# Second group's u moved and y stored by GpSimd instead of ScalarE, in a streaming encoder layer

## The chip, the cores and the metric

The kernel runs on one core of one Trainium2 chip. Its time is the device time of one execution in microseconds; a smaller number is better. The core has a matrix engine (PE), a vector engine (VectorE, DVE in the rows), a scalar engine (ScalarE, ACT), GpSimd (POOL) and a sync engine (SyncE, SP) that only issues DMAs. DMAs are issued from SP, ACT and POOL queues and carried out by 16 DMA engines that all share.

## The reference

One layer of a hybrid encoder on 512 prompt and 64 sample positions of 2048 features, all in float32:

```
q, k, v, u = split(x @ w_in)
att = rms_norm(band_attention(q, k, v))
ssm = rms_norm(s5(u))        # 64 groups of 16 channels, 64 complex states each; gelu and gate at the end
x1  = layer_norm(alpha * x + concat(att, ssm) @ w_out)
s   = einsum(x1 @ wq, keys)  # 8 heads, 2 halves, 128 keys: top 16 of each, top 16 of their sums
y   = (gelu(x1 . u_tab[idx]) * softmax(top)) @ v_tab[idx]    # 128 experts out of 16384 per position
x2  = layer_norm(alpha * x1 + y)
```

Outputs are x2, the new k and v rows and the last states.

## The kernel before

Positions are dealt into two groups: A with the 64 sample and 128 prompt positions, B with the other 384. Group A runs first, through projections, state space part, attention, w_out, layer norm (tiles 0 and 1) and the expert search. Then B runs the same stages on PE, while VectorE works on the experts of the finished tiles. Every engine has its program written out by hand, in a fixed order, with semaphores between them.

**Slabs.** PE multiplies by 128-column slabs of 1 MB of weights (`slab`, L1556), two buffers, two PSUM banks. SP loads them, in order, among its other loads; a slab waits for its weights and for the copy out of its bank two slabs before (`slab_out`). ScalarE makes these copies (`out_of`, `u_out`). At a width of 384 positions a slab takes about 10.3 us.

**Table rows.** An expert step gathers one row of 2048 float32 from `peer_u` or `peer_v` for each of 128 positions: 1 MB, one indirect DMA on GpSimd (`gather`, L592), one multiply on VectorE (`one_row`, L1360). `ROWS` numbers them 0 to 895. `ring()` gives each row a slot: two slots up to row 15, four from row 16, more later. `gather(i)` waits until the row before in its slot was used, so GpSimd runs two rows ahead of VectorE up to row 15 and four afterwards. VectorE's program has the rows at fixed places: two after each of heads 1 to 7 of tile 0 (`head`, L1265; rows 0 to 13), 28 rows (14 to 41), then one after each of 13 steps of the state scan of B (42 to 54), three ahead of each of the eight heads of tile 1 (55 to 78), 20 rows (79 to 98), and then the first use of y (L1466).

**u of group B.** The eight u slabs of B come as two before the 16 slabs of `N_WA` and six after. The PSUM result of a slab has channels on partitions; the state space matrices want (step, channel) on partitions. So ScalarE stores two slabs at a time to DRAM (`u_store`, L677, four parts) and reads each part back in another layout with eight copies of 48 KB, in runs of 48 numbers, 192 bytes (`u_move`, L682). PE waits for all of them (L1796) before the state products `s_pair`, which are dealt between the matmuls of slabs of v.

**y of group B.** `y_pair` makes y in PSUM between the matmuls of slabs of k and q. After each of four batches of eight pairs ScalarE copies to `U8B` (L931) and issues eight stores of the same shape (L939). SP waits for all 32 (L498) and loads y back as `yB` (L499, 1.5 MB) behind the slab `N_QB + 5`, whose load waits for slab `N_QB + 3`; VectorE waits for it at L1463.

The queue of GpSimd has the row gathers and nothing else in this part of the program.

Of the kernel before, what the change touches and what calls it, by code (L numbers as in the profile page):

```python
# [25 lines left out]
GRP, SG, SN = 64, 16, 64  # L26
SL = 8
# [8 lines left out]
NB = T - NA  # L36
# [32 lines left out]
N_UB = [48, 49, 66, 67, 68, 69, 70, 71]  # L69
N_MA, N_WA = 32, 50  # L70
N_VB, N_KB, N_QB = 72, 80, 88
# [31 lines left out]
def ring():  # L103

    held = [None] * len(SLOT_FROM)
    turns = [0] * len(SLOT_FROM)
    out = []
    for i in range(NR):
        free = [j for j in range(len(SLOT_FROM)) if i >= SLOT_FROM[j]]
        j = min(free, key=lambda j: (-1 if held[j] is None else held[j], j))  # L110
        turns[j] += 1
        out.append((j, turns[j], held[j]))
        held[j] = i
    return out


PLACE = ring()


PARTS = [(0, 0, KK), (1, 0, KK // 2), (2, 0, KK // 2), (2, KK // 2, KK // 2)]  # L120
# [33 lines left out]
def build(nc, a, o):  # L154
    ctx = ExitStack()
    with ctx:
# [405 lines left out]
        @block.gpsimd  # L562
        def _(pool):
            link = Chain(pool, pool_chain)

            pool.wait_ge(ext_done, 1)
            pool.dma_start(escr, ext).then_inc(ext_stored, 16)
            pool.wait_ge(zero_done, 1)
            pool.dma_start(kext.rearrange("(g a) h n -> (a h) g n", a=8)[:, :, 0:7 * SG],
                           zer.rearrange("p (g n) -> p g n", g=8)).then_inc(zeros_stored, 16)  # L570
            pool.wait_ge(ext_stored, 16)
            pool.wait_ge(zeros_stored, 16)
            pool.sem_inc(bias_done, 1)
            pool.wait_ge(tables, 1)
            for g in range(GP):
                wv = lambda t: t[:, :, g, :].unsqueeze(3).to_broadcast([P, 2, NW, SG])
                cvv = lambda t: t[:, g, :].unsqueeze(1).unsqueeze(1).to_broadcast([P, 2, NW, SG])
                if g >= 4:
                    pool.wait_ge(k_done, g - 3)
                    pool.wait_ge(ca_stored[g % 4], 16 * (g // 4))  # L580
                nc.gpsimd.tensor_tensor(tP[0], wv(WrNWi), cvv(Cr), ALU.mult)  # L581
                link(nc.gpsimd.tensor_tensor(tP[1], wv(NWiNWr), cvv(Ci), ALU.mult))
                link(nc.gpsimd.tensor_tensor(CAz[g % 4].rearrange("p r (k h) -> p r k h", k=NW), tP[0], tP[1], ALU.add))
                pool.sem_inc(ca_built, 1)
                link.zero()
            toeplitz(pool, 1)

            pool.wait_ge(y_stored[0], 16 * SL)
            pool.dma_start(yA.rearrange("p (m n) -> p m n", m=8), yscrA.rearrange("(m p) s c -> p m (s c)", p=P)
                           ).then_inc(y_moved[0], 16)  # L590

            def gather(i):  # L592
                kind, t, s = ROWS[i]
                j, turn, before = PLACE[i]
                if i < KK:
                    if s % TOPK == 0:
                        pool.wait_ge(idx_ready, s // TOPK + 1)
                elif s == 0 and kind == "u" or i == R_V3 or i == R_V4:
                    pool.wait_ge(idx_ready, PH + t)
                if before is not None:  # L600
                    pool.wait_ge(used, before + 1)
                elif j < 4:
                    pool.wait_ge(placed, 1)
                    pool.wait_ge(x1_stored, 32)
                    if j >= 2:
                        pool.wait_ge(idx_ready, PH)
                elif j == 4:
                    pool.wait_ge(placed, 2)
                    pool.wait_ge(x1_stored, 32)
                else:  # L610
                    pool.wait_ge(v_stored, 32)
                pool.indirect_dma_start(  # L612
                    out=slot[j], out_offset=None, in_=a["peer_" + kind],
                    in_offset=bass.IndirectOffsetOnAxis(ap=idx[:, t * KK + s:t * KK + s + 1], axis=0)
                    ).then_inc(got[j], 16)

            def e_products(e):
                q = e // EC
                if e % EC == 0 and q >= 4:
                    pool.wait_ge(act_ready, NACT + q - 3)  # L620
                pool.indirect_dma_start(  # L621
                    out=dots[:, 3 * KK + e:3 * KK + e + 1], out_offset=None, in_=ascr,
                    in_offset=bass.IndirectOffsetOnAxis(ap=idxe[:, e:e + 1], axis=0)).then_inc(e_got[q % 4], 16)

            def sum_store(k):
                pool.wait_ge(staged, k + 1)
                pool.dma_start(vscr[k], vstage).then_inc(v_stored, 16)

            for i in range(R_V3 - EAHEAD):
                gather(i)  # L630
                if i == R_V1 + 5:
                    sum_store(0)
                if i == R_U2 + 5:
                    sum_store(1)
            pool.wait_ge(idx_ready, PH + NT - 1)
            for b in range(2):
                pool.wait_ge(a_st[b], 16 * EB // 4)
            for k in range(EAHEAD):
                gather(R_V3 - EAHEAD + k)
                e_products(k)  # L640
            for k in range(NE):
                gather(R_V3 + k)
                if EAHEAD + k < NE:
                    e_products(EAHEAD + k)

        @block.scalar
        def _(act):
# [29 lines left out]
            def u_store(group, uP, uscr, count, lo, hi_, part):  # L677
                act.wait_ge(slab_out, count)
                act.dma_start(uscr.rearrange("(m p) s c -> p m (s c)", p=P)[:, lo:hi_],
                              uP[:, lo:hi_].rearrange("p m s c -> p m (s c)")).then_inc(u_stored[group][part], 16)  # L680
# [151 lines left out]
            def ln1_out(t):  # L832
                t0, n = TILES[t]
                ab, base, banks = (catA, 0, L[2:4]) if t < NGA else (catB, NA, L[0:2])
                for c in range(4):
                    act.wait_ge(x1t_done, 4 * t + c + 1)
                    nc.scalar.copy(half(ab, c)[:, :, t0 - base:t0 - base + n],
                                   banks[c % 2].rearrange("p (q t) -> p q t", q=4)[:, :, 0:n]).then_inc(x1t_out, 1)
                act.dma_start(x1scr[t], x1s[t]).then_inc(x1_stored, 16)
# [41 lines left out]
            def mixed_a(first):  # L881
                for i in range(16):
                    act.wait_ge(slab_done, first + i + 1)
                    src = L[(first + i) % 2]
                    nc.scalar.copy(mixA[:, i, 0:TS], src[:, 0:TS])
                    nc.scalar.copy(mixA[:, i, TS:TS + NA], src[:, 0:NA]).then_inc(slab_out, 1)
# [9 lines left out]
            ln1_stats(1)  # L896
            u_out(N_UB[1], 1, uPB, NB)
            ln1_out(1)
            mixed_a(N_WA)
            scores(0)  # L900
            scores(1)
# [2 lines left out]
            act.wait_ge(x1_ready, 2)  # L904
            for q in range(2, 8):
                u_out(N_UB[q], q, uPB, NB)
                if q == 2:
                    u_store(1, uPB, uscrB, N_UB[1] + 1, 0, 2, 0)
                elif q % 2:
                    u_store(1, uPB, uscrB, N_UB[q] + 1, q - 1, q + 1, q // 2)  # L910
                else:
                    u_move(1, uscrB, U8B, q - 4, q - 2, q // 2 - 2)
            out_of(N_VB, vB[:, 0, :], L[0][:, 0:NB])
            for part in (2, 3):
                u_move(1, uscrB, U8B, 2 * part, 2 * part + 2, part)
            for i in range(1, 4):
                out_of(N_VB + i, vB[:, i, :], L[i % 2][:, 0:NB])
            for b in range(8):
                act.wait_ge(s_done, GP + 4 * b + 4)
# [9 lines left out]
            for b in range(4):  # L929
                act.wait_ge(y_done[1], 8 * b + 8)  # L930
                nc.scalar.copy(U8B[:, 16 * b:16 * b + 16, :].rearrange("p (g a) c -> p a g c", a=2),  # L931
                               low[:, 1024:2048].rearrange("p (a n) -> p a n", a=2)[:, :, 0:8 * CB].rearrange(
                                   "p a (g c) -> p a g c", g=8)
                               ).then_inc(y_out[1], 1)
                if b < 2:
                    out_of(N_KB + 6 + b, kT[:, 6 + b, NA:T], L[b % 2][:, 0:NB])
                act.wait_ge(y_out[1], b + 1)
                for t in range(SL):
                    act.dma_start(yscrB.rearrange("(g h) s c -> s h g c", h=SG)[t][:, 16 * b:16 * b + 16, :],  # L939
                                  U8B[t * SG:(t + 1) * SG, 16 * b:16 * b + 16, :]).then_inc(y_stored[1], 16)  # L940
            for i in range(6):
                out_of(N_QB + i, qB[:, i, :], L[i % 2][:, 0:NB], DH ** -0.5)
            act.wait_ge(yd_ready, 2)
# [1024 lines left out]
```

## Time and profile before

| | |
|---|---|
| median of 3 timed runs | 3700.64 us (3700.53 to 3703.7) |
| the profiled execution, its own time | 3716.53 us |
| its span on the core | 3714.6 us |
| PE, VectorE, ScalarE, GpSimd busy | 66%, 74%, 9%, 33% |
| DMA moved | 1332.41 MB, mean 359 GB/s |
| granted TensorE clock, mean | 0.822 |

The busy share of an engine is an average over stages with different limits, so the stretch between 640 and 1160 us, where u is moved and y stored, is to be read by itself.

### The profile page before, as it was taken

The numbers are of one execution on the slowest core, as the hardware profiler recorded it, in microseconds if no ns is written. First come the engines' busy times: TensorE is split into PE (matmuls) and PEld (weight loads), VectorE is DVE, ScalarE is ACT, GpSimd is POOL, SyncE is SP. The second block draws the span as 40 slices with busy tenths as digits, with TensorE's granted clock in tenths as the row PEclk, the third lists the DMA queues.
The fourth block names the chain that finished last, engine by engine and source line by source line (L and its number), as shares of the span: only waits on it lengthen the run. The fifth ranks groups of instructions, "written<-read, shape, count | busy, mean of one in ns | idle before, by whom it ended". The sixth has DMA issues, their size and how long they took to land.

```text
span 3714.6 us, 30313 instructions
## 1 busy us (share of the span) xinstructions
PE 2464.5 (66%) x11208; PEld 1898.9 (51%) x11208; DVE 2764.5 (74%) x3210; ACT 332.5 (9%) x832; POOL 1237.7 (33%) x1273
## 2 busy tenths in 40 slices
PE   7798799987965776969989999999978000000000
PEld 7687689544733454545577878777767000000000
DVE  5331220979989997787789889985557999999988
ACT  1212211000002221001010000000000000000000
POOL 2420000122123332222222223222222577777772
PEclk9899899998986667989999999999999555555555
DMA  8774355898999999989999999999999999999998
GB/s 248 223 230 124 136 189 187 272 391 331 353 391 344 410 409 383 422 358 397 422 422 423 423 423 423 423 418 423 423 384 410 409 400 408 409 410 383 393 373 350
DMA packets 296882, 1332.41 MB, mean 359 GB/s; under 512 B 69728, under 2 KB 135808, under 8 KB 145312
## 3 DMA queue, kind: packets, MB, share of 16 engines
q0 software_dynamic: 138624, 945.22, 63.1%
q1 hardware_dynamic: 125376, 371.83, 27.1%
q10 hardware_dynamic: 32736, 13.44, 1.4%
q8 instruction: 89, 1.46, 0.2%
q14 instruction: 57, 0.47, 0.0%
HBM read 1282.60 MB, written 57.20 MB: 361 GB/s over the span
## 4 chain that ended last, share of the span: by engine, by line
PE 34%; DMA 25%; DVE 19%; POOL 9%; issue 9%; ACT 1%; SPq 1%; ACTq 1%; DVEq 0%; POOLq 0%
PE low L1561 18%; DMA arena<-in_ut 16%; PE low L1902 10%; DVE arena L1377 6%; POOL arena L612 5%; POOL arena L621 5%; DVE acc L1393 4%; DMA arena<-in_peer_v,arena 3%; DMA arena<-in_w 2%; DMA arena<-in_peer_u,arena 2%; PE low L1635 1%; PE acc L1635 1%; DMA arena<-y_scratch_b 1%; DVE low L1393 1%; DVE arena L1195 1%
## 5 line engine op out<-in xcount | busy, mean ns | idle before, releaser
L1393 DVE SCALAR_TENSOR_TENSOR acc<-arena,acc 128x2048 f32<-128x2048 f32 x443 | 1042.9, 2354 | 266.1 <-DMA arena<-in_peer_v,arena 229.1
L1561 PE MATMUL low<-arena 128*128 128x192 f32 (+1 forms) x4096 | 1063.2, 419 | 102.1 <-DMA arena<-in_w 76.8
L1902 PE MATMUL low<-arena 128*128 128x256 f32 x4096 | 908.8, 383 | 103.3 <-DMA arena<-in_ut 103.2
L1561 PEld LDWEIGHTS low<-arena 128*128 128x128 f32 x4096 | 736.0, 195 | 378.4 <-DMA arena<-in_w 74.4
L1902 PEld LDWEIGHTS low<-arena 128*128 128x128 f32 x4096 | 781.3, 192 | 230.6 <-DMA arena<-in_ut 109.8
L612 POOL DMA_INDIRECT arena<-in_peer_v,arena x576 | 573.4, 995 | 909.2 <-DVE acc L1393 740.9
L1377 DVE SCALAR_TENSOR_TENSOR arena<-arena,acc 128x2048 f32<-128x2048 f32 x320 | 725.0, 2285 | 118.4 <-DMA arena<-in_peer_u,arena 110.9
L612 POOL DMA_INDIRECT arena<-in_peer_u,arena x320 | 320.0, 1000 | 1197.3 <-DVE arena L1377 862.4
L1393 DVE SCALAR_TENSOR_TENSOR low<-arena,low 128x2048 f32<-128x2048 f32 x126 | 296.6, 2354 | 29.6 <-issue 13.6
L621 POOL DMA_INDIRECT arena<-expert_scratch,arena x256 | 260.7, 1018 | 79.2 <-issue 79.2
L873 ACT COPY arena<-low 128x256 f32<-128x256 f32 x128 | 47.6, 372 | 957.5 <-DMA expert_scratch<-arena 635.3
L1687 PE MATMUL low<-arena 128*128 128x128 f32 x320 | 78.9, 403 | 72.3 <-DVE arena L1204 65.2
L1687 PEld LDWEIGHTS low<-arena 128*128 128x128 f32 x320 | 62.8, 283 | 121.1 <-DVE arena L1204 114.0
L1259 DVE MAX8 arena<-arena 128x8 f32<-128x128 f32 (+1 forms) x120 | 40.5, 338 | 97.8 <-ACT arena L847 94.8
L1195 DVE CUSTOM_DVE_ANT_0 arena<-acc,arena 128x128 f32<-128x128 f32 (+1 forms) x24 | 10.6, 447 | 114.4 <-PE acc L1665 78.5
L670 ACT COPY arena<-low 128x384 f32<-128x384 f32 (+1 forms) x80 | 34.3, 430 | 620.4 <-PE low L1561 598.5
L1109 DVE TENSOR_TENSOR arena<-arena 128x256 f32<-128x256 f32 x32 | 15.5, 484 | 99.1 <-PE acc L1608 98.6
L1240 DVE SCALAR_TENSOR_TENSOR arena<-arena,acc 128x2048 f32<-128x2048 f32 x2 | 4.6, 2289 | 98.3 <-PE acc L1748 98.3
L1671 PE MATMUL low<-arena 64*128 64x256 f32 (+2 forms) x96 | 66.8, 797 | 13.6 <-DVE arena L1195 9.6
L1713 PE MATMUL low<-arena 128*64 128x128 f32 x320 | 73.3, 388 | 0.0
L865 ACT ACTIVATE arena<-arena 128x16 f32<-128x16 f32 x16 | 3.5, 216 | 682.2 <-DMA arena<-expert_scratch,arena 391.6
L581 POOL TENSOR_TENSOR arena<-arena 128x288 f32<-128x288 f32 x32 | 22.6, 705 | 112.2 <-DMA c_scratch<-arena 83.1
(274 smaller groups left out, 1688.0 us busy)
## 6 DMA issues: line engine op xcount, KB each, us to landing
arena<-in_w SPq DMA_DIRECT2D x128, 1024.0 KB
arena<-in_ut SPq DMA_DIRECT2D x128, 1024.0 KB
expert_scratch<-arena SPq DMA_DIRECT2D x64, 256.0 KB
arena<-in_peer_v,arena POOLq DMA_INDIRECT x576
arena<-toeplitz_scratch SPq DMA_DIRECT2D x64, 128.0 KB, 4.1
arena<-c_scratch SPq DMA_DIRECT2D x64, 128.0 KB, 4.7
bias_scratch<-distance_scratch SPq DMA_DIRECT2D x1, 5120.0 KB, 23.2
x_scratch<-arena ACTq DMA_DIRECT2D x5, 1024.0 KB
```

What stands on the lines that cost most here:

```text
L612: pool.indirect_dma_start(out=slot[j], out_offset=None, in_=a["peer_" + kind], in_offset=bass.IndirectOffsetOnAxis(ap=idx[:, t * KK + s:t ...
L621: pool.indirect_dma_start(out=dots[:, 3 * KK + e:3 * KK + e + 1], out_offset=None, in_=ascr, in_offset=bass.IndirectOffsetOnAxis(ap=idxe[: ...
L873: nc.scalar.copy(astg[j // 2 % 2].rearrange("p u (i t) -> p i u t", i=2)[:, j % 2], L[j % 4][:, 0:NSD].rearrange("p (u t) -> p u t", u=2)) ...
L1195: nc.vector.tensor_tensor_reduce(S[0:rows, 0:keys], src, bias, -1.0, HIGHEST, ALU.add, ALU.min, accum_out=stat[0:rows, 0:1]).then_inc(mn_r ...
L1377: stt(slot[j], slot[j], 1.0, acc[:, :], ALU.mult, ALU.mult, accum_out=dots[:, t * KK + s:t * KK + s + 1]).then_inc(used, 1)
L1393: stt(held, slot[j], wv_, held, ALU.mult, ALU.add).then_inc(used, 1)
L1561: ins = mm(L[n % 2][:, 0:width], wring[n % 2][:, k, :], rhs(k), start=k == 0, stop=k == KT - 1)
L1635: ins = mm(d, CAy[g % 8][hf(g2), r, :], Hs[hf(g2), r, g, 0:width], start=False, stop=r == 1)
L1671: ins = mm(L[u % 2][:, 0:n], qB[hf(hh), m, P * (j - 1):P * j], kT[hf(hh), m, TS:TS + n], start=True, stop=True)
L1687: ins = mm(L[2][:, P * k:P * k + P], S[:, P * k:P * k + P], dg, start=True, stop=True)
L1713: ins = mm(d, vs, PT[:, P * k:P * k + P], start=k == 0, stop=k == j)
L1902: ins = mm(L[j % 4][:, 0:NSD], ud[j % 4][:, k, :], lane(catB, k)[:, P:NB], start=k == 0, stop=k == KT - 1)
```

## The change

GpSimd gets two functions, `u_move(part)` and `y_store(b)`, and calls them at set places of its loop over rows: part 0 of u ahead of row 0, parts 1, 2 and 3 ahead of rows 2, 4 and 8, and the four batches of y ahead of rows 70, 77, 84 and 91. ScalarE no longer issues these 64 copies. Its store of part 0 of u moves up, behind the second layer norm; the stores of parts 1 to 3 stay behind the copies of slabs 3, 5 and 7 of u.

```diff
--- before.py
+++ after.py
@@ -115,6 +115,10 @@
 
 
 PLACE = ring()
+
+
+U_ROWS = [2, 4, 8]
+Y_ROWS = [70, 77, 84, 91]
 
 
 PARTS = [(0, 0, KK), (1, 0, KK // 2), (2, 0, KK // 2), (2, KK // 2, KK // 2)]
@@ -589,6 +593,20 @@
             pool.dma_start(yA.rearrange("p (m n) -> p m n", m=8), yscrA.rearrange("(m p) s c -> p m (s c)", p=P)
                            ).then_inc(y_moved[0], 16)
 
+            def u_move(part):
+                pool.wait_ge(u_stored[1][part], 16)
+                pool.wait_ge(x1_ready, 2)
+                for k in range(SL):
+                    pool.dma_start(U8B[k * SG:(k + 1) * SG, 16 * part:16 * part + 16],
+                                   uscrB.rearrange("(g h) s c -> s h g c", h=SG)[SL - 1 - k][:, 16 * part:16 * part + 16]
+                                   ).then_inc(u_moved[1], 16)
+
+            def y_store(b):
+                pool.wait_ge(y_out[1], b + 1)
+                for t in range(SL):
+                    pool.dma_start(yscrB.rearrange("(g h) s c -> s h g c", h=SG)[t][:, 16 * b:16 * b + 16, :],
+                                   U8B[t * SG:(t + 1) * SG, 16 * b:16 * b + 16, :]).then_inc(y_stored[1], 16)
+
             def gather(i):
                 kind, t, s = ROWS[i]
                 j, turn, before = PLACE[i]
@@ -626,7 +644,12 @@
                 pool.wait_ge(staged, k + 1)
                 pool.dma_start(vscr[k], vstage).then_inc(v_stored, 16)
 
+            u_move(0)
             for i in range(R_V3 - EAHEAD):
+                if i in U_ROWS:
+                    u_move(U_ROWS.index(i) + 1)
+                if i in Y_ROWS:
+                    y_store(Y_ROWS.index(i))
                 gather(i)
                 if i == R_V1 + 5:
                     sum_store(0)
@@ -896,6 +919,7 @@
             ln1_stats(1)
             u_out(N_UB[1], 1, uPB, NB)
             ln1_out(1)
+            u_store(1, uPB, uscrB, N_UB[1] + 1, 0, 2, 0)
             mixed_a(N_WA)
             scores(0)
             scores(1)
@@ -904,16 +928,9 @@
             act.wait_ge(x1_ready, 2)
             for q in range(2, 8):
                 u_out(N_UB[q], q, uPB, NB)
-                if q == 2:
-                    u_store(1, uPB, uscrB, N_UB[1] + 1, 0, 2, 0)
-                elif q % 2:
+                if q % 2:
                     u_store(1, uPB, uscrB, N_UB[q] + 1, q - 1, q + 1, q // 2)
-                else:
-                    u_move(1, uscrB, U8B, q - 4, q - 2, q // 2 - 2)
-            out_of(N_VB, vB[:, 0, :], L[0][:, 0:NB])
-            for part in (2, 3):
-                u_move(1, uscrB, U8B, 2 * part, 2 * part + 2, part)
-            for i in range(1, 4):
+            for i in range(4):
                 out_of(N_VB + i, vB[:, i, :], L[i % 2][:, 0:NB])
             for b in range(8):
                 act.wait_ge(s_done, GP + 4 * b + 4)
@@ -934,10 +951,6 @@
                                ).then_inc(y_out[1], 1)
                 if b < 2:
                     out_of(N_KB + 6 + b, kT[:, 6 + b, NA:T], L[b % 2][:, 0:NB])
-                act.wait_ge(y_out[1], b + 1)
-                for t in range(SL):
-                    act.dma_start(yscrB.rearrange("(g h) s c -> s h g c", h=SG)[t][:, 16 * b:16 * b + 16, :],
-                                  U8B[t * SG:(t + 1) * SG, 16 * b:16 * b + 16, :]).then_inc(y_stored[1], 16)
             for i in range(6):
                 out_of(N_QB + i, qB[:, i, :], L[i % 2][:, 0:NB], DH ** -0.5)
             act.wait_ge(yd_ready, 2)
```

GpSimd's order where row gathers begin (`in_peer_u` gathers, the first two being rows 0 and 1; `u_scratch_b` copies are the moves of u; in brackets the semaphores waited for), before:

```order
L589 DMA arena<-y_scratch_a 128x8x192 [waits y_stored_a]
L612 DMA arena<-in_peer_u,arena 128x2048 [waits x1_stored,x1_placed,idx_ready]
L612 DMA arena<-in_peer_u,arena 128x2048 [waits x1_stored,x1_placed]
L612 DMA arena<-in_peer_u,arena 128x2048 [waits row_used] x14
L612 DMA arena<-in_peer_u,arena 128x2048 [waits x1_stored,idx_ready,x1_placed]
L612 DMA arena<-in_peer_u,arena 128x2048 [waits idx_ready,x1_stored,x1_placed]
```

and in the changed kernel:

```order
L593 DMA arena<-y_scratch_a 128x8x192 [waits y_stored_a]
L600 DMA arena<-u_scratch_b 16x16x48 [waits x1_ready,u_stored_b0]
L600 DMA arena<-u_scratch_b 16x16x48 x7
L630 DMA arena<-in_peer_u,arena 128x2048 [waits x1_stored,x1_placed,idx_ready]
L630 DMA arena<-in_peer_u,arena 128x2048 [waits x1_stored,x1_placed]
L600 DMA arena<-u_scratch_b 16x16x48 [waits x1_ready,u_stored_b1]
L600 DMA arena<-u_scratch_b 16x16x48 x7
L630 DMA arena<-in_peer_u,arena 128x2048 [waits row_used] x2
L600 DMA arena<-u_scratch_b 16x16x48 [waits x1_ready,u_stored_b2]
L600 DMA arena<-u_scratch_b 16x16x48 x7
L630 DMA arena<-in_peer_u,arena 128x2048 [waits row_used] x4
L600 DMA arena<-u_scratch_b 16x16x48 [waits x1_ready,u_stored_b3]
```

The sixteen rows stood in one run; now moves stand ahead of rows 0, 2, 4 and 8, and each part first waits for its store, `u_stored_b`.

GpSimd's order further on, from row 64 (the single gathers with `idx_ready` are rows 64, 80 and 96, the first of a head's sixteen), before:

```order
L612 DMA arena<-in_peer_u,arena 128x2048 [waits row_used,idx_ready]
L612 DMA arena<-in_peer_u,arena 128x2048 [waits row_used] x15
L612 DMA arena<-in_peer_u,arena 128x2048 [waits row_used,idx_ready]
L612 DMA arena<-in_peer_u,arena 128x2048 [waits row_used] x15
L612 DMA arena<-in_peer_u,arena 128x2048 [waits row_used,idx_ready]
```

and in the changed kernel (`y_scratch_b` copies are the stores of y):

```order
L630 DMA arena<-in_peer_u,arena 128x2048 [waits row_used,idx_ready]
L630 DMA arena<-in_peer_u,arena 128x2048 [waits row_used] x5
L607 DMA y_scratch_b<-arena 16x16x48 [waits y_out_b]
L607 DMA y_scratch_b<-arena 16x16x48 x7
L630 DMA arena<-in_peer_u,arena 128x2048 [waits row_used] x7
L607 DMA y_scratch_b<-arena 16x16x48 [waits y_out_b]
L607 DMA y_scratch_b<-arena 16x16x48 x7
L630 DMA arena<-in_peer_u,arena 128x2048 [waits row_used] x3
L630 DMA arena<-in_peer_u,arena 128x2048 [waits row_used,idx_ready]
L630 DMA arena<-in_peer_u,arena 128x2048 [waits row_used] x3
L607 DMA y_scratch_b<-arena 16x16x48 [waits y_out_b]
L607 DMA y_scratch_b<-arena 16x16x48 x7
```

Before there were only gathers here; now a group of eight stores stands ahead of rows 70, 77 and 84 (and another, not shown, ahead of row 91), each behind a wait for ScalarE's copy of y.

ScalarE's order from the copy of slab 5 of u, before (`arena<-low` are its copies out of PSUM):

```order
L670 COPY arena<-low 128x384 [waits slab_done]
L679 DMA u_scratch_b<-arena 128x2x384 [waits slab_out]
L670 COPY arena<-low 128x384 [waits slab_done]
L685 DMA arena<-u_scratch_b 16x16x48 [waits u_stored_b1]
L685 DMA arena<-u_scratch_b 16x16x48 x7
L670 COPY arena<-low 128x384 [waits slab_done]
L679 DMA u_scratch_b<-arena 128x2x384 [waits slab_out]
L670 COPY arena<-low 128x384 [waits slab_done]
L685 DMA arena<-u_scratch_b 16x16x48 [waits u_stored_b2]
L685 DMA arena<-u_scratch_b 16x16x48 x7
L685 DMA arena<-u_scratch_b 16x16x48 [waits u_stored_b3]
L685 DMA arena<-u_scratch_b 16x16x48 x7
```

and now:

```order
L693 COPY arena<-low 128x384 [waits slab_done] x2
L702 DMA u_scratch_b<-arena 128x2x384 [waits slab_out]
L693 COPY arena<-low 128x384 [waits slab_done] x2
L702 DMA u_scratch_b<-arena 128x2x384 [waits slab_out]
L693 COPY arena<-low 128x384 [waits slab_done] x4
L937 COPY arena<-low 128x4x2x48 [waits s_done] x2
L693 COPY arena<-low 128x384 [waits slab_done]
L937 COPY arena<-low 128x4x2x48 [waits s_done] x2
```

The moves and their waits are gone, and the copies and stores follow each other.

## Rows read from the trace of the kernel before

**Rows 1.** DMA view: busy share in 40 slices; issues, KB each, us to landing.

```profile
DMA  8774355898999999989999999999999999999998
...
arena<-in_ln_g SPq DMA_DIRECT2D x3, 1024.0 KB, 4.7
```

**Rows 2.** Busy time by stretch; columns as in the header line.

```profile
core 0: us, PE busy (x) PEld busy (x) DVE busy (x) ACT busy (x) POOL busy (x), PEclk, DMA share, GB/s
...
680.00:720.00 40.00, 40.00 (x125) 23.56 (x124) 37.04 (x102) 1.92 (x4) 5.62 (x6) 1.00 0.85 273
760.00:800.00 40.00, 35.19 (x213) 18.55 (x214) 27.58 (x25) 3.38 (x7) 12.39 (x14) 0.91 1.02 413
...
1200.00:1300.00 100.00, 74.54 (x256) 48.54 (x256) 98.50 (x155) 22.81 (x57) 34.67 (x37) 0.62 0.99 402
1500.00:1600.00 100.00, 100.00 (x312) 58.92 (x311) 71.82 (x31) 6.32 (x12) 28.27 (x31) 1.00 1.01 422
```

**Rows 3.** Chain of work, pieces in order of time, 600 to 1160 us.

```profile
753.89 2.31 DVE arena L1377 x2
...
849.66 0.86 DVE arena L1134
...
923.39 0.91 PE low L1561 x2
...
1059.16 34.31 DMA arena<-y_scratch_b
```

**Rows 4.** Timeline of VectorE: rows 84, 98, and the first use of y.

```profile
1045.18 2.29 DVE L1377 SCALAR_TENSOR_TENSOR arena<-arena,acc 128x2048 f32<-128x2048 f32 x1 [1.47 <-DMA arena<-in_peer_u,arena]
...
1088.54 2.29 DVE L1377 SCALAR_TENSOR_TENSOR arena<-arena,acc 128x2048 f32<-128x2048 f32 x1 [0.79 <-DMA arena<-in_peer_u,arena]
...
1093.49 2.21 DVE L1466 SCALAR_TENSOR_TENSOR arena<-arena 128x384 f32<-128x384 f32 x4 [2.65 <-DMA arena<-y_scratch_b]
```

**Rows 5.** Timeline of ScalarE with its DMA issues (ACTq), 660 to 745 us.

```profile
671.75 0.38 ACTq L679 DMA_DIRECT2D u_scratch_b<-arena  x1
...
692.39 0.38 ACTq L679 DMA_DIRECT2D u_scratch_b<-arena  x1
...
713.03 0.42 ACTq L679 DMA_DIRECT2D u_scratch_b<-arena  x1
...
722.85 15.81 ACTq L685 DMA_DIRECT2D arena<-u_scratch_b  x16
```

**Rows 6.** Timeline of ScalarE: last y copy, its DMA issues, next copy.

```profile
1024.06 10.45 ACTq L939 DMA_DIRECT2D y_scratch_b<-arena  x8
1034.55 0.87 ACT L672 ACTIVATE arena<-low 128x384 f32<-128x384 f32 x2 [10.52 <-issue]
```

**Rows 7.** Tensor u_scratch_b: issue to landing of its stores, min/median/max.

```profile
DMA to landing us min/median/max: 8.2/9.3/11.0
```

**Rows 8.** Timeline of GpSimd: issues of small copies and row gathers.

```profile
211.86 8.95 POOL L367 DMA_DIRECT2D toeplitz_scratch<-kernel_scratch  x16 [6.74 <-DMA kernel_scratch<-arena]
...
656.94 1.03 POOL L612 DMA_INDIRECT arena<-in_peer_u,arena  x1 [311.81 <-DVEq L1327]
...
669.56 0.94 POOL L612 DMA_INDIRECT arena<-in_peer_u,arena  x1 [10.31 <-DVE arena L1377]
```

**Rows 9.** Timeline of GpSimd: row gathers 83, 84 and 91.

```profile
1034.88 0.94 POOL L612 DMA_INDIRECT arena<-in_peer_u,arena  x1 [8.25 <-DVE arena L1377]
1037.09 0.94 POOL L612 DMA_INDIRECT arena<-in_peer_u,arena  x1 [1.27 <-DVE arena L1377]
...
1056.11 0.94 POOL L612 DMA_INDIRECT arena<-in_peer_u,arena  x1 [2.47 <-DVE arena L1377]
```

**Rows 10.** Timeline of VectorE: rows 2 and 4 of the first head stage.

```profile
681.48 2.29 DVE L1377 SCALAR_TENSOR_TENSOR arena<-arena,acc 128x2048 f32<-128x2048 f32 x1 [0.24 <-DVE arena L1325]
...
695.96 2.29 DVE L1377 SCALAR_TENSOR_TENSOR arena<-arena,acc 128x2048 f32<-128x2048 f32 x1 [0.24 <-DVE arena L1325]
```

**Rows 11.** Timeline of PE: the first state product.

```profile
754.34 0.44 PE L1806 MATMUL low<-arena 128*64 128x48 f32 x8
```

## Prediction

> **What bounds the kernel now.** I read the DMA view first. The busy share of the DMA engines is at 9 in nearly every slice after the first two fifths [rows 1]. The windows then say what kind of stretch each one is [rows 2]. From 680 to 720 us VectorE is busy 37.0 of 40 us and DMA 0.85: the first head stage (top-16 search, decode, and two table rows after each of heads 1 to 7) is VectorE's. From 760 to 800 DMA is at 1.02 and VectorE at 27.6 of 40: gathers and weights share the bandwidth. From 1200 to 1300 VectorE is busy 98.5 of 100 with DMA at 0.99, and from 1500 to 1600 DMA is at 1.01: the later stages have no slack on one of the two. All that follows the first group is one long VectorE program with the table rows dealt into it in fixed places, so a microsecond that VectorE loses before 1160 us comes back only where gathers are the limit and somebody else gave them bandwidth.
>
> The chain of work between 750 and 1160 us has four parts [rows 3]: VectorE ends rows 12 and 13 at 756.2, then takes rows 14 to 41 as they land, until 849.66 (93.5 us for 28 rows, 3.3 us each, where one multiply takes 2.3); VectorE's scan steps run from 849.66 until the state is ready, when PE starts the y pairs at 923.39; last stands the load of y, 34.31 us from 1059.16. VectorE waited for that load only 2.65 us [rows 4].
>
> The copies that the change moves cost nobody else much today. ScalarE issues the moves of u between its copies; the longest piece is sixteen issues, 15.81 us from 722.85 [rows 5], while PE has two banks ahead. Only the last eight stores of y hurt: their issue holds ScalarE from 1024.06 for 10.45 us, and the copy that frees PE's bank starts at 1034.55 after 10.52 us of idleness by issue [rows 6].
>
> **The change part by part.** Removed from ScalarE: 32 moves and 32 stores. Added to GpSimd, in order, among the row gathers: eight moves ahead of row 0, then ahead of rows 2, 4 and 8, and eight stores ahead of rows 70, 77, 84 and 91. GpSimd works in order, so a gather behind a move also waits for what the move waits for.
>
> Part 0 of u is stored ahead of the sixteen slabs that come before the first head stage, and row 0 is gathered only at 656.94 [rows 8]: nothing lost. Part 1 is not stored until ScalarE has copied slab 3: the store is issued at 671.75 [rows 5] and lands 9.3 us later, the median of four (8.2 to 11.0) [rows 7], at 681.1. Only then can GpSimd issue the eight moves. A plain copy of 256 short pieces on GpSimd shows as 8.95 us for sixteen, 0.56 each [rows 8]: 4.5 us, until 685.6. Gather 2, which before was issued at 669.56 [rows 8], starts then. From issue to the multiply that needs it I take 8.1 us, from gather 84 (issued at 1037.09 [rows 9], multiply at 1045.18 after a wait for it [rows 4]). Row 2 starts at 693.7 instead of 681.48 [rows 10]: 12.2 us late.
>
> Part 2 does not depend on that delay, since PE and ScalarE run on: store issued at 692.39, landed at 701.7, moves issued by 706.2, gather 4 landed at 714.3. Row 4 started at 695.96 before [rows 10]: **18.3 us late**, and this contains the 12.2. In this stage only two slots take rows, so nothing is fetched ahead and VectorE stands. Bounds of this term: lowest 692.39 + 8.2 + 4.5 + 4.7 (a load of 1 MB into SBUF, alone in its queue [rows 1]) = 709.8, 13.8 us late; highest 692.39 + 11.0 + 7.5 (eight at a gather's 0.94) + 10.1 (gather 0, issued at 656.94 [rows 8], was there for its row at 667.0, 14.48 before row 2) = 721.0, 25.0 us late.
> Part 3: store at 713.03, landed 722.3, moves issued by 726.8. Gather 8 has to wait for row 6 anyway, which starts one step (695.96 - 681.48 = 14.5 us) after row 4, at 728.8. It costs nothing; without that cover it would be up to 4.5.
>
> A rule to weigh here: the row says that a gather of 1 MB takes 8.1 us to its use, beside other traffic [rows 4, 9]. The Trainium skill, page "DMA: Bandwidth & Descriptors", section "Anatomy of one DMA — SWDGE (gpsimd) path", gives a fixed 2.0 us plus the bytes at 436 GB/s, an estimate of 4.4 us for this gather. With it row 4 would be 14.6 us late instead of 18.3. The row was taken in a saturated stretch and this stage has 0.85, so the truth may lie between; the sum keeps the row.
>
> Is it taken back? PE has its moved u in time (part 3 is issued by 726.8, and the first state product ran at 754.34 [rows 11]), so PE starts the state products on time and draws its slabs and tables 18 us ahead of VectorE. In the stretch of 28 rows the demand beside the gathers is then a little higher: PE could have up to 3 MB more done by row 41, and 3 MB at the stretch's 413 GB/s [rows 2] are 7 us. Lower bound 0, if the queues share as before and 3.3 us per row stays. I take **+2 us** (nearer to 0, since PE waits for weights there too). VectorE then reaches the scan about 20 us late, the state is ready about 20 us late, and PE's y pairs start late by the same.
>
> The stores of y, in times that leave out this shift. GpSimd idles 8.25 us between triples of gathers in the second head stage [rows 9], which hides the 4.5 us of the first two groups of stores (rows 70, 77); uncovered they would cost 4.5 each. The third group is issued behind gather 83, from 1035.8 to 1040.3, so gather 84 goes 3.2 us later than at 1037.09 [rows 9], and its row has waited for it before [rows 4]: about 3 us. The fourth stands ahead of gather 91. GpSimd idled 2.47 us before that one at 1056.11 [rows 9], so it is issued from 1053.6 + 3 to 1061, and lands behind the gathers in front of it, 8.1 us on, near 1069.5. The y load can start then, 10 us later than its 1059.16. On the other side ScalarE is free at 1024.06, PE runs its next slabs 10.5 us earlier, and the 1 MB slab issued just before the y load is out of its queue. If the 34.31 us were for 1 + 1.5 MB, the 1.5 MB alone take 20.6: y lands between 1090 and 1104, middle 1097. Row 98 ended near 1090.8 [rows 4], now near 1094. VectorE starts on y at 1097 instead of 1093.49: **+3 us** (from -3, the old wait gone, to +11).
>
> Sum: 18.3 + 2 + 3 = 23 us. Behind it VectorE and PE are both late at the same point of the program and nothing in the later stages is idle enough to absorb it. The profiled execution took 3716.5 us and its span 3714.6; it is 15.9 us above the median of 3700.64 of the timed runs. So 3739.5 in a profiled run, and 3700.6 + 23 = **3723 us** in timed ones.
>
> **Rivals.**
> 1. *Likeliest: the late gathers 2 and 4.* Bounds 13.8 + 0 - 3 = +11 to 25 + 7 + 11 = +43; with the terms not all at one end, +12 to +33, so 3713 to 3734. Chance 0.63.
> 2. *The stall is taken back in rows 14 to 41, and PE's 10.5 us are a gain.* One mechanism: while VectorE stands, PE's side gets its tables and slabs, and the gathers then find the bandwidth free. It decides from where 28 rows take 93.5 - 18.3 = 75 us or less, 2.7 us each; the floor is 2.3, so it is possible. Then VectorE is on time, the y wait of 2.65 us goes, and part of PE's 10.5 us fills DMA time: 0 to -7 us, 3694 to 3700. Against it: DMA is at 1.02 there, the amount to be moved is the same, and from 754 to 773 the engines would be partly idle, which nothing refunds. Faster than by 0.2%: 0.08. Taken back in part, so that it ends within 7.4 us: 0.11.
> 3. *y comes later still:* the last stores queue behind four gathers, land near 1080, and the y load again takes 34 us, to 1114. VectorE has only two rows to do meanwhile. 18 + 2 + 20 = +40, 3735 to 3745. For it: the y load was slow beside gathers [rows 3]. Against it: GpSimd stops gathering when VectorE stands, which frees the bandwidth. Chance 0.12.
> 4. *Short landings:* the moves and gathers in the half-empty stage take 5 us rather than 8, and the y part costs nothing: +8 to +12, 3709 to 3713. Chance 0.06.
>
> **How the numbers follow.** Slower by over 0.2% (7.4 us, about what a measurement of this kernel can tell): 0.63 + 0.12 + 0.06 = 0.81; within it 0.11; faster 0.08. The range goes from 3704, which takes in half of the partly absorbed cases, to 3740, which takes in half of rival 3; some 0.12 is left out by the chances of the cases, and the rest of the two tenths stands for unknown costs inside them.
>
> **What would show it.** GpSimd: a wait of about 22 us ahead of the moves before gather 2, ended by the store of u, and gather 2 near 686, gather 4 near 706. VectorE: idle before rows 2 and 4, together 18 us (14 to 25), none before rows 6 and 8; scan near 870 instead of 849.66; PE's first y pair near 943. ScalarE: no idleness by issue at 1034. The y load issued about 30 us after its old time, shorter than 34 us, and VectorE's wait for it 3 to 10 us. The forecast is wrong if gather 2 is not held by the store, if rows 14 to 41 take under 80 us, or if the lateness at 1160 is not found at the end.

## The result, and the profile after

The changed kernel takes 3719.75 us (median of 6 runs, 3714.09 to 3725.89) against 3702.26 us (6 runs, 3700.53 to 3707.18): ratio 1.0045 (95% interval 1.0032 to 1.0058), so 16.7 us slower (12 to 21). Its profiled execution took 3725.89 us, span 3723.9.

Timeline of GpSimd in the changed kernel, first head stage (start and length in us; in brackets the idle time before and what ended it). L600 are moves of u, L630 row gathers. It is to be read against [rows 8]; this execution runs 1.5 us later than that of before from the start of the stage (first search of head 0 at 648.31 instead of 646.77).

```profile
679.65 4.56 POOL L600 DMA_DIRECT2D arena<-u_scratch_b  x8 [18.87 <-DMA u_scratch_b<-arena]
684.51 1.01 POOL L630 DMA_INDIRECT arena<-in_peer_u,arena  x1 [0.30 <-issue]
...
703.09 4.57 POOL L600 DMA_DIRECT2D arena<-u_scratch_b  x8 [16.28 <-DMA u_scratch_b<-arena]
707.96 1.01 POOL L630 DMA_INDIRECT arena<-in_peer_u,arena  x1 [0.30 <-issue]
...
726.82 4.56 POOL L600 DMA_DIRECT2D arena<-u_scratch_b  x8 [6.26 <-DMA u_scratch_b<-arena]
732.17 1.02 POOL L630 DMA_INDIRECT arena<-in_peer_u,arena  x1 [0.80 <-DVE arena L1390]
```

The stores it waits for land after 6.1, 8.9 and 12.0 us, against 8.2 to 11.0 in [rows 7] (DMA view of three short windows, KB each, us to landing):

```profile
u_scratch_b<-arena ACTq DMA_DIRECT2D x1, 384.0 KB, 6.1
```

```profile
u_scratch_b<-arena ACTq DMA_DIRECT2D x1, 384.0 KB, 8.9
```

```profile
u_scratch_b<-arena ACTq DMA_DIRECT2D x1, 384.0 KB, 12.0
```

GpSimd waits 18.87 us for the store of part 1 and 16.28 us for that of part 2, with gathers 2 and 4 queued behind. It had idled there before too (10.31 us before gather 2 [rows 8]), so the loss is less than the wait: gather 2 goes 13.4 us late (684.51 against 669.56, less the 1.5). VectorE in the same stage, rows 2, 4 and 6, against [rows 10]:

```profile
691.50 2.29 DVE L1390 SCALAR_TENSOR_TENSOR arena<-arena,acc 128x2048 f32<-128x2048 f32 x1 [8.65 <-DMA arena<-in_peer_u,arena]
...
714.17 2.29 DVE L1390 SCALAR_TENSOR_TENSOR arena<-arena,acc 128x2048 f32<-128x2048 f32 x1 [8.08 <-DMA arena<-in_peer_u,arena]
...
729.33 2.29 DVE L1390 SCALAR_TENSOR_TENSOR arena<-arena,acc 128x2048 f32<-128x2048 f32 x1 [0.24 <-DVE arena L1338]
```

It stands 8.65 us before row 2 and 8.08 us before row 4, where it had 0.24 before, and does not stand before row 6. In the windows the stretch that had VectorE at 37.0 of 40 us [rows 2] now has 21.4, and DMA 0.75 instead of 0.85:

```profile
680.00:720.00 40.00, 40.00 (x126) 23.57 (x125) 21.40 (x52) 1.92 (x4) 14.06 (x22) 1.00 0.75 243
760.00:800.00 40.00, 40.00 (x263) 21.24 (x262) 30.15 (x54) 3.37 (x7) 10.41 (x12) 1.00 0.92 351
```

In this trace nothing of it comes back in rows 14 to 41: the first scan step (in [rows 3] at 849.66) is at 868.64, so 17.4 us later beside the 1.5. The third and fourth group of stores of y (L607) and the gathers behind them, against [rows 9]:

```profile
1053.80 0.94 POOL L630 DMA_INDIRECT arena<-in_peer_u,arena  x1 [8.24 <-DVE arena L1390]
1054.74 1.80 POOL L607 DMA_DIRECT2D y_scratch_b<-arena  x3
1057.38 2.78 POOL L607 DMA_DIRECT2D y_scratch_b<-arena  x5 [0.83 <-issue]
1060.46 1.00 POOL L630 DMA_INDIRECT arena<-in_peer_u,arena  x1 [0.30 <-DVE arena L1390]
...
1076.11 0.94 POOL L630 DMA_INDIRECT arena<-in_peer_u,arena  x1 [2.47 <-DVE arena L1390]
1077.05 4.56 POOL L607 DMA_DIRECT2D y_scratch_b<-arena  x8
1081.91 1.01 POOL L630 DMA_INDIRECT arena<-in_peer_u,arena  x1 [0.30 <-issue]
```

Gather 84 is issued at 1060.46, and VectorE waits 5.28 us for it where it waited 1.47 [rows 4]. Below are row 84, row 98 and the first use of y (1114.11, L1479). It has no bracket: VectorE does not wait for y any more, and row 98 before it is the one that comes late.

```profile
1067.64 2.29 DVE L1390 SCALAR_TENSOR_TENSOR arena<-arena,acc 128x2048 f32<-128x2048 f32 x1 [5.28 <-DMA arena<-in_peer_u,arena]
...
1111.90 2.29 DVE L1390 SCALAR_TENSOR_TENSOR arena<-arena,acc 128x2048 f32<-128x2048 f32 x1 [1.29 <-DMA arena<-in_peer_u,arena]
1114.11 2.20 DVE L1479 SCALAR_TENSOR_TENSOR arena<-arena 128x384 f32<-128x384 f32 x4
```

The y load goes at 1087.55, 28.4 us after its old time [rows 3]; SP has been waiting since 1068.7 for the stores. It lands 26.1 us after its issue (34.3 before), near 1113.7, only 0.5 us ahead of its use. ScalarE's 10.52 us of idleness by issue [rows 6] are gone.

```profile
1068.30 0.43 SPq L501 DMA_DIRECT2D out_h<-arena  x1
1087.55 0.38 SPq L503 DMA_DIRECT2D arena<-y_scratch_b  x1
```

To follow a lateness through the program I take the start of one gather in each profile, less the start of the first search of head 0 (646.77 before, 648.31 here), and subtract the same of before. Gather 756 is issued at 3311.8 before and 3335.2 here: 2686.9 - 2665.0 = 21.9 us late. It had been 21.1 at gather 224 (1463.8 and 1486.4): what is late there is still late almost 2000 us further on. The profiled executions end only 9.4 us apart because that of before lost 14 us behind gather 756 (373.5 us to the last gather, 359.4 in the changed kernel) in code that is the same; its 3716.53 us lie above all other timed runs of before (3707.18 at most).

### The profile page after: what moved, and what is told of

Its sections match the earlier page's. It is cut to its first block, busy times and chain, and to the rows that moved or that the text cites. A ratio compares the mean times of both kernels' runs of the same rounds, so it can differ in the third digit from the quotient of the medians.

```text
span 3723.9 us, 30317 instructions
## 1 busy us (share of the span) xinstructions
PE 2473.7 (66%) x11208; PEld 1905.9 (51%) x11208; DVE 2764.5 (74%) x3210; ACT 333.1 (9%) x832; POOL 1247.5 (33%) x1337
## 4 chain that ended last, share of the span: by engine, by line
PE 33%; DMA 32%; DVE 22%; POOL 6%; issue 5%; ACT 1%; ACTq 0%; SPq 0%; DVEq 0%; POOLq 0%
PE low L1574 18%; DMA arena<-in_ut 17%; PE low L1915 10%; DMA arena<-in_peer_v,arena 9%; DVE arena L1390 8%; DMA arena<-in_peer_u,arena 3%; DVE acc L1406 3%; POOL arena L630 3%; POOL arena L639 3%; DMA arena<-in_w 2%; DVE low L1406 1%; PE acc L1648 1%; DVE arena L1208 1%; DMA arena<-bias_scratch 1%; PE acc L1621 1%
## 5 line engine op out<-in xcount | busy, mean ns | idle before, releaser
L630 POOL DMA_INDIRECT arena<-in_peer_v,arena x576 | 561.4, 975 | 926.0 <-DVE acc L1406 788.2
L630 POOL DMA_INDIRECT arena<-in_peer_u,arena x320 | 320.9, 1003 | 921.1 <-DVE arena L1390 806.1
L639 POOL DMA_INDIRECT arena<-expert_scratch,arena x256 | 245.2, 958 | 78.3 <-issue 78.3
L600 POOL DMA_DIRECT2D arena<-u_scratch_b x32 | 18.1, 592 | 258.1 <-DMA u_scratch_b<-arena 258.1
L1684 PE MATMUL low<-arena 64*128 64x256 f32 (+2 forms) x96 | 69.7, 829 | 12.4 <-DVE arena L1208 8.4
## 6 DMA issues: line engine op xcount, KB each, us to landing
expert_scratch<-arena SPq DMA_DIRECT2D x64, 256.0 KB, 26.1
```

Of the source, the lines that this page charges most:

```text
L630: pool.indirect_dma_start(out=slot[j], out_offset=None, in_=a["peer_" + kind], in_offset=bass.IndirectOffsetOnAxis(ap=idx[:, t * KK + s:t ...
L639: pool.indirect_dma_start(out=dots[:, 3 * KK + e:3 * KK + e + 1], out_offset=None, in_=ascr, in_offset=bass.IndirectOffsetOnAxis(ap=idxe[: ...
L1684: ins = mm(L[u % 2][:, 0:n], qB[hf(hh), m, P * (j - 1):P * j], kT[hf(hh), m, TS:TS + n], start=True, stop=True)
```

## The experiments

Each was compared with the kernel before on the same chip, 6 to 12 runs against 27 to 29. The table gives the lateness in us against the profile of before, worked out as above, at the issue of four gathers, at the first scan step, at the issue of the y load, and at "y use", VectorE's first instruction on y. Each column but the last comes from one profiled execution:

| run | gather 16 | first scan step | gather 84 | gather 91 | y load | y use | gather 756 | timed ratio (95%) |
|---|---|---|---|---|---|---|---|---|
| changed kernel | 17.8 | 17.4 | 21.8 | 24.3 | 26.8 | 19.1 | 21.9 | 1.0045 (1.0032 to 1.0058) |
| e1, u only | 15.7 | 13.9 | 13.9 | 12.2 | 14.1 | 14.2 | 14.9 | 1.0043 (1.0028 to 1.0059) |
| e6, u part 1 only | 9.6 | 9.5 | 9.4 | 7.8 | 9.8 | 9.9 | 13.9 | 1.0030 (1.0018 to 1.0042) |
| e2, y only | 0.0 | 0.1 | 5.0 | 9.4 | 11.7 | 3.7 | 7.4 | 1.0012 (1.0001 to 1.0023) |
| e8, y, third group at 80 | -0.1 | 0.1 | 0.0 | 4.0 | 7.4 | -0.8 | 0.8 | 0.9998 (0.9984 to 1.0013) |
| e3, u at 4, 8, 10 | 0.4 | 0.7 | 4.8 | 8.2 | 10.0 | 1.9 | 2.9 | 1.0006 (0.9995 to 1.0016) |
| e7, copies first | -0.1 | 0.1 | 0.0 | 2.9 | -12.8 | 2.9 | 2.2 | 0.9999 (0.9989 to 1.0009) |

**e1_u_only.** The changed kernel with the stores of y given back to ScalarE:

```diff
             for i in range(R_V3 - EAHEAD):
...
-                if i in Y_ROWS:
-                    y_store(Y_ROWS.index(i))
...
+                act.wait_ge(y_out[1], b + 1)
+                for t in range(SL):
+                    act.dma_start(yscrB.rearrange("(g h) s c -> s h g c", h=SG)[t][:, 16 * b:16 * b + 16, :],
+                                  U8B[t * SG:(t + 1) * SG, 16 * b:16 * b + 16, :]).then_inc(y_stored[1], 16)
```

> The changed kernel with the stores of y back on ScalarE; only the moves of u are on GpSimd, ahead of rows 0, 2, 4 and 8. Theory (VectorE stands before rows 2 and 4 because the moves wait for u's stores): the whole stall of the changed kernel is here, 8 to 9 us before row 2 and about 8 before row 4, gather 84 late by 17 to 18 us; ScalarE's 10.5 us of idleness by issue is back. Time 17 us (12 to 21) above the kernel before, ratio 1.0046. Rival (the loss of the changed kernel is made mostly by the stores of y on GpSimd): under 7 us above.

Measured 3719.69 against 3706.59 us, ratio 1.0043 (1.0028 to 1.0059): 16 us by the ratio. VectorE stands 9.09 us before row 2 and 6.12 before row 4:

```profile
688.28 2.29 DVE L1392 SCALAR_TENSOR_TENSOR arena<-arena,acc 128x2048 f32<-128x2048 f32 x1 [9.09 <-DMA arena<-in_peer_u,arena]
...
708.90 2.29 DVE L1392 SCALAR_TENSOR_TENSOR arena<-arena,acc 128x2048 f32<-128x2048 f32 x1 [6.12 <-DMA arena<-in_peer_u,arena]
```

The moves of u make most of the loss; the rival with under 7 us falls. The times can't tell this run from the changed kernel (1.0043 and 1.0045). Of the 15.7 us at gather 16 it has 13.9 left at the first scan step, so here rows 14 to 41 gave 1.8 us back.

**e6_part1_only.** As e1, with parts 2 and 3 where their stores have landed:

```diff
-U_ROWS = [2, 4, 8]
+U_ROWS = [2, 8, 10]
```

> The moves of u on GpSimd ahead of rows 0, 2, 8 and 10, the stores of y on ScalarE: of the two stalls only the one of part 1 is left. Theory: VectorE waits 8 to 9 us before row 2 and not before row 4, and the lateness of 8 to 9 us stays to the end: ratio 1.0023 (1.0012 to 1.0035). Rival (a lateness of this size in the head stage is taken back while rows 14 to 41 wait for DMA): under 3 us.

Measured 3715.86 against 3704.4 us, ratio 1.0030 (1.0018 to 1.0042), 11 us. VectorE's rows 2 and 4:

```profile
691.66 2.29 DVE L1392 SCALAR_TENSOR_TENSOR arena<-arena,acc 128x2048 f32<-128x2048 f32 x1 [9.25 <-DMA arena<-in_peer_u,arena]
...
706.39 2.29 DVE L1392 SCALAR_TENSOR_TENSOR arena<-arena,acc 128x2048 f32<-128x2048 f32 x1 [0.24 <-DVE arena L1340]
```

One stall of 9.25 us before row 2, and 0.24 before row 4. Gather 16 is 9.6 us late and the first scan step 9.5, so rows 14 to 41 give nothing back here though they wait for DMA. Gather 756 is 13.9 us late, not 9.9 as the use of y. Of these 4 us, 2.6 come between gathers 200 and 224 (10.2 and 12.8 late), and so do 1.6 in the changed kernel, 3.3 in e2 and 2.3 in e10, while e1, e3 and e4 lose nothing there. Why is not settled, so lateness behind gather 200 is good to some 3 us only.

**e3_u_late.** The changed kernel with one list of numbers changed:

```diff
-U_ROWS = [2, 4, 8]
+U_ROWS = [4, 8, 10]
```

> The changed kernel with the moves of parts 1, 2 and 3 ahead of rows 4, 8 and 10 in place of 2, 4 and 8, where the store has landed before GpSimd comes there (or nearly: part 3's store lands near 724, gather 10 goes at 727.5). Theory: no wait of VectorE before rows 2 to 13 beyond 1 us, so only the cost of y stays: +2 to +6 us, as the run with y only. Rival (it is the eight issues and the packets on the gathers' queue that cost, not the wait for the store): each moved group still costs 4 to 5 us, +12 to +18 us.

Measured 3706.89 against 3706.59 us, ratio 1.0006 (0.9995 to 1.0016), which is 2 us (-2 to +6). The moves of part 1 still wait for the store, but with gathers 2 and 3 ahead of them:

```profile
682.19 4.55 POOL L600 DMA_DIRECT2D arena<-u_scratch_b  x8 [8.68 <-DMA u_scratch_b<-arena]
687.05 1.01 POOL L630 DMA_INDIRECT arena<-in_peer_u,arena  x1 [0.30 <-DVE arena L1390]
```

Gather 4 goes 2.2 us later than before and VectorE does not stand before any of the rows 2 to 13. The same 24 issues are on the same queue, so the issues and their packets cost nothing that these runs can resolve: the wait for the store did. The rival with 4 to 5 us a group falls.

**e2_y_only.** The kernel before with `y_store` and its call as in the changed kernel, and ScalarE's stores taken out:

```diff
+Y_ROWS = [70, 77, 84, 91]
...
             for i in range(R_V3 - EAHEAD):
+                if i in Y_ROWS:
+                    y_store(Y_ROWS.index(i))
                 gather(i)
```

> The kernel before with only the stores of y on GpSimd, ahead of rows 70, 77, 84 and 91. Theory: gather 84 late by about 4 us, the y load issued some 5 to 10 us later than at 1059, VectorE late by 2 to 5 us at 1160; time +2 to +6 us, ratio 1.0005 to 1.0016. Rival (ScalarE's freed 10.5 us are a gain for PE that reaches the end): -3 to -7 us.

Measured 3710.38 against 3706.59 us, ratio 1.0012 (1.0001 to 1.0023), 4.4 us. Below are gather 83, the third group and gather 84 on GpSimd, then rows 83 and 84 (L1384) and the first use of y (L1473) on VectorE:

```profile
1040.13 0.94 POOL L621 DMA_INDIRECT arena<-in_peer_u,arena  x1 [9.57 <-issue]
1041.07 4.56 POOL L598 DMA_DIRECT2D y_scratch_b<-arena  x8
1045.93 1.01 POOL L621 DMA_INDIRECT arena<-in_peer_u,arena  x1 [0.30 <-issue]
```

```profile
1048.94 2.29 DVE L1384 SCALAR_TENSOR_TENSOR arena<-arena,acc 128x2048 f32<-128x2048 f32 x1 [3.79 <-DMA arena<-in_peer_u,arena]
...
1053.15 2.29 DVE L1384 SCALAR_TENSOR_TENSOR arena<-arena,acc 128x2048 f32<-128x2048 f32 x1 [1.91 <-DMA arena<-in_peer_u,arena]
...
1101.01 2.20 DVE L1473 SCALAR_TENSOR_TENSOR arena<-arena 128x384 f32<-128x384 f32 x4 [0.34 <-DMA arena<-y_scratch_b]
```

VectorE waits 3.79 us for row 83 and 1.91 for row 84, with more at the rows behind, and 0.34 for y where it had been 2.65 [rows 4]. Gather 83 stands ahead of the group and is yet 1.4 us late; the profile names no cause for that. Row 98 starts 6.0 us late and VectorE's use of y comes 3.7 us late, the difference being most of the old wait for y. The y load takes 26.2 us and lands at the end of row 98, within 0.4 us, so late rows are enough for nearly all of the loss.

**e8_y_third_at_80.** As e2, the third group four rows earlier, into the 8 us that GpSimd idles between triples:

```diff
-Y_ROWS = [70, 77, 84, 91]
+Y_ROWS = [70, 77, 80, 91]
```

> The kernel before with the stores of y on GpSimd ahead of rows 70, 77, 80 and 91: the third group stands in GpSimd's idle time ahead of a triple of gathers instead of between gathers 83 and 84. Theory (the cost of y on GpSimd is that gathers 84 to 98 go late while VectorE takes rows as fast as they land): gather 84 on time within 1 us, gather 91 late only by the fourth group; total cost 2 to 3 us less than with 84, so 0 to +3 us against the kernel before. Rival (the cost is that the y load goes later): no change from the run with 84, +4 us.

Measured 3703.01 against 3704.4 us, ratio 0.9998 (0.9984 to 1.0013). The group, gather 80 behind it, and gather 84, which it held up in e2:

```profile
1016.55 0.63 POOL L598 DMA_DIRECT2D y_scratch_b<-arena  x1
1018.50 3.91 POOL L598 DMA_DIRECT2D y_scratch_b<-arena  x7 [1.32 <-issue]
1025.33 1.00 POOL L621 DMA_INDIRECT arena<-in_peer_u,arena  x1 [2.92 <-DVE arena L1384]
...
1040.59 0.94 POOL L621 DMA_INDIRECT arena<-in_peer_u,arena  x1 [1.27 <-DVE arena L1384]
```

Gather 84 is on time, and VectorE comes to y 0.8 us early instead of 3.7 late. The y load still goes 7.4 us late (11.7 in e2), takes 26.1 us, and costs nothing: the rival falls. This rests on the profiles; the timed intervals of e2 and e8, taken on two chips, overlap.

**e7_copies_first.** The kernel before, where ScalarE frees PE's banks before its last eight issues:

```diff
+                if b == 3:
+                    for i in range(2):
+                        out_of(N_QB + i, qB[:, i, :], L[i % 2][:, 0:NB], DH ** -0.5)
                 act.wait_ge(y_out[1], b + 1)
...
-            for i in range(6):
+            for i in range(2, 6):
```

> The kernel before with one edit: ScalarE copies the first two q slabs out before it issues the last eight stores of y. Theory (DMA is the limit there, so PE's 10.5 us are worth only the DMA time left idle, 0.10 of 40 us, and VectorE's wait of 2.65 us): PE's next slab starts 10 us earlier and the time falls by 0 to 4 us. Rival (PE's chain to the y load is the limit): -6 to -10 us.

Measured 3703.21 against 3704.4 us, ratio 0.9999 (0.9989 to 1.0009).

```profile
1021.33 0.50 ACT L672 ACTIVATE arena<-low 128x384 f32<-128x384 f32 x1
...
1021.71 0.50 ACT L672 ACTIVATE arena<-low 128x384 f32<-128x384 f32 x1
1021.87 10.16 ACTq L942 DMA_DIRECT2D y_scratch_b<-arena  x7
1032.57 0.49 ACT L672 ACTIVATE arena<-low 128x384 f32<-128x384 f32 x1 [10.36 <-PE low L1564]
```

Both copies are made ahead of seven of the eight issues, PE's next slab is out at 1032.57 (before: 1048.0, this execution being 2.7 us early), and SP issues the y load 12.8 us earlier. VectorE nevertheless comes to y 2.9 us later: gathers 96 to 98 now take 12.0 to 13.8 us from issue to multiply, where they took 9.1 to 9.7, with DMA at 1.02 from 1050 to 1090 in both. That fits a y load that takes its bandwidth from the gathers. The 10.5 us that ScalarE's issues cost PE were worth nothing here: -0.4 us (-4 to +3).

**e4_both_rows**, **e10_both_rows_again**: the changed kernel with both lists changed; **e5_y_early_only**, **e11_y_early_again**: e2 with the early list of y.

```diff
-U_ROWS = [2, 4, 8]
-Y_ROWS = [70, 77, 84, 91]
+U_ROWS = [4, 8, 10]
+Y_ROWS = [65, 71, 77, 83]
```

> As the last, and the stores of y ahead of rows 65, 71, 77 and 83, each the first place where its batch has been copied. Theory: the last stores are issued near 1027 to 1032 instead of behind gather 90, the y load can go when slab N_QB + 3 is done, at about 1048 instead of 1059, VectorE's wait of 2.65 us for y is gone and DMA is used while PE would have stood: -2 to -7 us against the kernel before. Rival (stores of y in the gathers' queue delay rows wherever they stand): 0 to +4 us.

> The kernel before with the stores of y on GpSimd ahead of rows 65, 71, 77 and 83, the moves of u on ScalarE as before. Theory (as in the run with both rows moved, where DMA work is conserved and an earlier y load only takes bandwidth from the gathers): within 4 us of the kernel before, -1 us. Rival (the moves of u on GpSimd cost some us there and hid a gain of the early y): -4 to -7 us.

> The kernel with u ahead of rows 4, 8, 10 and y ahead of 65, 71, 77, 83 once more, on one chip with the next. It measured 0.9997 before. Theory: it and the next differ only in who issues the moves of u, off everybody's path, so they agree within 4 us. Rival: the 8 us between their two measurements are real and come again.

> The kernel before with the stores of y on GpSimd ahead of rows 65, 71, 77 and 83 once more. It measured 1.0019 (1.0009 to 1.0029) on another chip. Theory: within 4 us of the run beside it, so near 1.000 to 1.001. Rival: 1.002 again, with the run beside it at 0.9997: then the moves of u on ScalarE cost 8 us when y is stored early.

Ratios: e4 0.9997 (0.9987 to 1.0007), e5 1.0019 (1.0009 to 1.0029), and again e10 1.0006 (0.9995 to 1.0017), e11 1.0003 (0.9991 to 1.0015). The y load goes 12.4 us early in e4, as expected, but the gain of 2 to 7 us expected there is a miss: VectorE is at y 3.2 us later than before, as in e7, and e4 and e10 measured -1 and +2 us. e5's 7 us (3 to 11) were a miss too, against -1 within 4. e4 and e5 were measured on two chips; side by side on one, as e10 and e11, they do not differ.

**e9_repaired.** The changed kernel with the moves where the stores have landed and the stores of y in GpSimd's idle time:

```diff
-U_ROWS = [2, 4, 8]
-Y_ROWS = [70, 77, 84, 91]
+U_ROWS = [4, 8, 10]
+Y_ROWS = [70, 77, 80, 91]
```

> The changed kernel with two rows of numbers changed: moves of u ahead of rows 4, 8 and 10, stores of y ahead of rows 70, 77, 80 and 91. Theory (all of the changed kernel's loss is in the places, not in the queue): each stall is gone, and it runs as the kernel before, ratio 0.999 to 1.001; so 16 to 17 us less than the changed kernel. Rival (64 copies on the gathers' queue cost something wherever they stand): +4 us or more.

Measured 3720.88 us against 3720.49 for the kernel before beside it (all kernels of this round were slower), ratio 0.9995 (0.9982 to 1.0007): no difference from the kernel before. Its single profile shows nothing at row 2 or row 4 and 0.2 us of lateness at gather 84, but 8.2 us at gather 756, most of it behind gather 588 (2.9); the timed runs show no such loss (-7 to +3 us), and its cause is open. No version was found that beats the kernel before.

## Why the prediction was right

It said 3723 us and +23; measured were 3719.75 and +16.7. The profile has 21.9 us of lateness, but its execution is the longest of the six, 6.1 us above their median. By its steps:

- *The moves wait for u's stores, with the gathers behind them.* Shown by GpSimd's wait of 18.87 us, by e3, which takes it away and most of the loss with it, and by e6, which leaves one of the two stalls (9.5 us at the first scan step, 11 timed). The term was 18.3 us; row 4 starts 16.7 us late, row 5 and the first scan step 17.4. Row 2 was to be 12.2 us late and was 8.5. Inside the term the pieces were off: the store of part 1 landed after 6.1 us and not 9.3, the eight issues took 4.56 (4.5), and the gathers were there after 7.0 and 6.2 us, not 8.1. The 8.1 came from a stretch with DMA at 1.01; this stage had 0.85 [rows 2] and fell to 0.75, as there are no gathers while GpSimd waits. The Trainium skill's fixed cost plus bytes ("DMA: Bandwidth & Descriptors", "Anatomy of one DMA — SWDGE (gpsimd) path") gave an estimate of 4.4; the rows lie between it and mine. Part 3 cost nothing, as predicted, but its store took 12.0 us: its moves were out only 0.8 us before gather 8 could go, so its cover was nearly used up.
- *+2 us while rows 14 to 41 share DMA.* Measured 0 in the changed kernel (gather 16 17.8 us late, scan step 17.4) and in e6, -1.8 in e1; so my lower bound of 0 was not quite low enough. PE did draw ahead: ScalarE copied slab N_VB + 6 out at 800.9 instead of 809.3.
- *+3 us by y.* The use of y is 19.1 us late where the scan step was 17.4, so 1.7 us; in e2 it is 3.7, and 4.4 timed. Between the times of the changed kernel and e1 no cost of y can be made out. The size was near, the place was not: I had VectorE wait 3 to 10 us for y. It waits for row 84 behind the third group of stores, and row 98 is 21.8 us late; from this the old wait of 2.65 us for y comes off. The y load took 26.1 us, inside my 20.6 to 34.3, and was in time by 0.5 us. e8 shows that with the third group elsewhere the cost is gone.
- *PE's 10.5 us.* The prediction used them only to take a slab out of the y load's way and counted no gain of their own. e7 confirms that there is none.
- *All of it reaches the end.* Confirmed within the noise: 21.1, 21.8 and 21.9 us at gathers 224, 300 and 756. The 2 us on top of the 19.1 at the use of y come mostly between gathers 200 and 224, as in e6, which has no stores of y on GpSimd. The timed 16.7 us lie 5 us lower than the profile, with an interval that holds 21 at its edge; e1 and e2 add up to 20 us timed. How many of these last few us are real is not settled.

Rival 2 (the stall is taken back) would have needed 75 us for 28 rows; they took 93.6, counted as in the prediction. (Its 756.2 is the end of row 12 alone; row 13 starts at 756.11 and ends near 758.4, so 28 rows took some 91 us before and after.) Rival 3 had y as what decides, with a load of 34 us; the load took 26.1 and, though issued at 1087.55, was in time. The first term makes up most of the sum and is what made the forecast right; that the y term came near owes something to luck, as the piece that decides was another.

## What to carry to other kernels

An in-order queue that runs ahead of its consumer by only two transfers has little room for a wait. Here the gathers of the first head stage were issued 11.9 us ahead of their multiply and needed 6 to 9: one that went 2.2 us late was free (e3), one that went 13.4 us late cost 8.65. So before putting a copy among such transfers, find when its source is ready and how many of them are then already issued. Moving the moves of u by two to four places took the ratio from 1.0045 to 1.0006 (e3). And in a stretch where DMA is busy all the time, setting an engine free earlier need not help: in e7 and e4 the y load went 12 to 13 us earlier, the gathers beside it took longer, and VectorE came to y 3 us later.

## What was not expected of the hardware

The same copies make fewer DMA packets when GpSimd issues them. Queues in the DMA view of the kernel before:

```profile
q0 software_dynamic: 138624, 945.22, 63.1%
...
q10 hardware_dynamic: 32736, 13.44, 1.4%
```

and of the changed kernel:

```profile
q0 software_dynamic: 140672, 948.37, 63.0%
...
q10 hardware_dynamic: 15328, 10.29, 0.9%
```

ScalarE's queue (q10) has 17408 packets fewer for 64 copies, 272 each, and GpSimd's (q0) 2048 more, 32 each, for the same 3.15 MB in runs of 192 bytes. The share of the 16 engines' span that q10's packets took falls from 1.4% to 0.9% while q0's stays (63.1 and 63.0), but no run here shows that the program gets shorter by it.
